# Modulation lines later, router rows turned without their gains, and six unread products between logits and first expert

## The reference

```python
mod_x = (jax.nn.silu(c) @ w_ada[l] + b_ada[l])[:, None, :]
sh_a, sc_a, g_a, sh_m, sc_m, g_m = jnp.split(mod_x, N_MOD, axis=-1)
...
x = x + g_a * _merge(ya, yb, ga, gb, w_oa[l], w_ob[l], w_out[l])
hx = _modulate(_rmsnorm(x, norm_mlp[l]), sh_m, sc_m)   # h * (1 + scale) + shift
x = x + g_m * moe(hx.reshape(b * s, d)).reshape(b, s, d)

def _moe(h, router_w, router_b, w_gate, b_gate, w_up, b_up, w_down, b_down):
    logits = (h @ router_w + router_b).astype(jnp.float32)
    top_logit, top_e = lax.top_k(logits, TOP_K)
    top_w = jax.nn.softmax(top_logit, axis=-1)
    ...
    gate = jnp.minimum(xe @ w_gate[e] + b_gate[e], SWIGLU_LIMIT)
    up = jnp.clip(xe @ w_up[e] + b_up[e], -SWIGLU_LIMIT, SWIGLU_LIMIT)
    act = (up + 1) * (gate * jax.nn.sigmoid(SWIGLU_ALPHA * gate))
    return act @ w_down[e] + b_down[e]
```

## Time and profile before

| | |
|---|---|
| median of three executions | 1819.28 us (1817.63 to 1820.83) |
| profiled execution | 1815.5 us |
| its span on the device | 1813.7 us |
| PE busy | 1748.5 us, 96% |
| DVE busy | 787.1 us, 43% |
| ACT busy | 571.7 us, 32% |
| DMA | 563.07 MB, mean 310 GB/s |
| chain that ended last | PE 77%, DMA 16%, DVE 4%, ACT 2% |

### The profile page before, as it was taken

How to read it: one execution, slowest core, us unless ns; L and a number is a source line. 1 busy time by engine, 2 the same in 40 slices (tenths; PEclk the granted TensorE clock), 3 DMA queues, 4 the chain that set the end, 5 groups by cost and what they waited for, 6 DMA issues and landing times.

```text
span 1813.7 us, 22741 instructions
## 1 busy us (share of the span) xinstructions
PE 1748.5 (96%) x9326; PEld 1032.5 (57%) x9326; DVE 787.1 (43%) x1419; ACT 571.7 (32%) x1034; POOL 20.6 (1%) x59
## 2 busy tenths in 40 slices
PE   6999999999999999999999999989999999999999
PEld 4988886333333333333332333348788888888887
DVE  3887964111111111111111111134677776767776
ACT  4546663101101101101010010135654446664443
POOL 1020010000000000000000000000000000000000
PEclk9999999999999999999999999999999999999999
DMA  8655478999999999999999999996235637425550
GB/s 319 232 199 211 174 286 332 414 430 431 430 431 430 431 430 431 429 432 429 431 430 431 431 431 430 431 390 226 102 137 205 212 119 276 139 94 186 186 198 34
DMA packets 122042, 563.07 MB, mean 310 GB/s; under 512 B 7216, under 2 KB 53424, under 8 KB 97360
## 3 DMA queue, kind: packets, MB, share of 16 engines
q1 hardware_dynamic: 121104, 558.70, 76.2%
q10 hardware_dynamic: 832, 2.89, 0.4%
HBM read 560.52 MB, written 1.05 MB: 310 GB/s over the span
## 4 chain that ended last, share of the span: by engine, by line
PE 77%; DMA 16%; DVE 4%; ACT 2%; issue 1%; SPq 0%; DVEq 0%; ACTq 0%
PE ps L1117 17%; PE ps L1140 10%; PE ps L1397 9%; PE ps L669 7%; PE ps L671 7%; PE ps L670 7%; DMA ring<-in_w_up 7%; DMA arena<-in_w_up 7%; PE ps L1398 4%; PE ps L1073 3%; PE ps L1054 3%; DVE part L2099 1%; DMA ring<-in_w_ada 1%; PE ps L994 1%; PE ps L1066 1%
## 5 line engine op out<-in xcount | busy, mean ns | idle before, releaser
L2099 DVE TENSOR_TENSOR part<-ring,part 128x1024 fp32r<-128x1024 f32 (+2 forms) x300 | 320.9, 1088 | 140.7 <-ACT part L1526 140.1
L669 PE MATMUL ps<-part,part 128*128 128x512 f32 (+1 forms) x888 | 312.5, 352 | 4.5 <-DVE part L2099 2.2
L671 PE MATMUL ps<-part,part 128*128 128x512 f32 (+1 forms) x888 | 301.9, 340 | 0.0
L670 PE MATMUL ps<-part,part 128*128 128x512 f32 (+1 forms) x888 | 301.8, 340 | 0.0
L1526 ACT ACTIVATE part<-ring 128x1024 fp32r<-128x1024 f32 (+2 forms) x299 | 272.9, 946 | 86.5 <-DVE ring L2099 69.6
L1117 PE MATMUL ps<-ring,arena 128*64 128x512 f32 x1216 | 268.3, 594 | 8.0 <-DMA ring<-in_w_up 8.0
L1397 PE MATMUL ps<-part,part 128*128 128x512 f32 x704 | 250.3, 398 | 0.0
L2096 DVE TENSOR_SCALAR arena<-ps 128x512 f32<-128x512 f32 x64 | 44.3, 692 | 421.2 <-PE ps L1117 421.2
L1398 PE MATMUL ps<-part,part 128*128 128x256 f32 x704 | 197.5, 281 | 0.0
L1117 PEld LDWEIGHTS ps<-ring,arena 128*64 128x64 f32 x1216 | 85.0, 137 | 188.1 <-issue 171.5
L669 PEld LDWEIGHTS ps<-part,part 128*128 128x128 f32 x888 | 168.3, 190 | 32.6 <-issue 7.8
(11 more groups left out here) (275 smaller groups left out, 1446.1 us busy)
## 6 DMA issues: line engine op xcount, KB each, us to landing
ring<-in_w_down SPq DMA_DIRECT2D x39, 2048.0 KB, 31.4
ring<-in_w_up SPq DMA_DIRECT2D x38, 2048.0 KB, 32.2
ring<-in_w_gate SPq DMA_DIRECT2D x38, 2048.0 KB, 31.4
arena<-in_w_up SPq DMA_DIRECT2D x26, 2048.0 KB, 33.7
ring<-in_ffn_w_in SPq DMA_DIRECT2D x44, 1024.0 KB, 7.6
arena<-in_w_down SPq DMA_DIRECT2D x18, 2048.0 KB, 32.6
spare<-in_w_gate SPq DMA_DIRECT2D x13, 2048.0 KB, 31.5
arena<-in_w_gate SPq DMA_DIRECT2D x13, 2048.0 KB, 31.4
```

The source lines that it names most:

```text
L669: e.matmul(out, x[0], y[0], start=first, stop=False, skip_group_check=True)
L670: e.matmul(out, x[0], y[1], start=False, stop=False, skip_group_check=True)
L671: return e.matmul(out, x[1], y[0], start=False, stop=last, skip_group_check=True)
L2099: return e.tensor_tensor(out, x, y, op)
```

## The change

Six things change, all before or at the start of the expert loop.

1. ada_first: slab 6 begins with block 14 instead of 11, slab 7 with 17 instead of 14, slabs 8 to 11 one block later each. ada_column stays.
2. The two heads of a unit share one operation for the negated maximum and one for the inverted sum; ACT waits once for the pair.
3. The rows of X are turned by PE without any gain (turn_x, 16 transposes of 128x128 by the identity), between the products of the out-projection. Scale and root are moved elsewhere: the router's weights are multiplied by the scale on DVE, the shift's part of the logits is made by eight products of its own (shift_logits) and added to the bias, and the logits are multiplied by root when they are picked. The products with the diagonal, the 16 turns into b.htok and their copies are gone.
4. Gathering takes X itself, with root in S instead of 1. Expert 0 is gathered as the others are, and its rows turned by transposes. Scale and shift are applied where the gathered rows leave PSUM, four instructions on ACT and four on DVE (gathered_right) for each expert, with gains laid out by 16 small products (slot_gains).
5. Six products which no instruction reads (stay_busy: identity times X into PS[2], 512 columns, the first 256) stand between the logits and the first expert's products.
6. mod and smcol are laid ahead of the ring, with a pad behind them, so that ring and arena move by 1,024 and 128 bytes a partition; the largest count is reduced after the selection for expert 0; a table of functions is loaded in block 36 for the logarithm and exponential in place of the square root, and the load of that table in the router goes.

```diff
-        ada_first = {4: 5, 5: 8, 6: 11, 7: 14, 8: 19, 9: 22, 10: 25, 11: 28}
+        ada_first = {4: 5, 5: 8, 6: 14, 7: 17, 8: 20, 9: 23, 10: 26, 11: 29}
...
-                for r in range(2):
-                    x = st(2 * u + r)
-                    e.wait_ge(*s_max.of("max", u, r))
-                    stt(x[1], x[0], -1.0, unit_rr(u, r), ALU.mult, ALU.mult).then_inc(*s_max.up(u, r))
+                e.wait_ge(*s_max.of("max", u, 1))
+                stt(st_pair(u, 1), st_pair(u, 0), -1.0, unit_rr(u, 0, 2), ALU.mult, ALU.mult).then_inc(*s_max.up(u))
...
+        mod = sb("mod", [128, 96])
+        smcol = sb("smcol", [128, 128])
+        sb("to_a_line", [128, -nc.sbuf_base % 256 // 4])
         ringt = sb("ring", [128, NSLOT, SLOT])
...
+            def turn_x(q, h):
+                e.wait_ge(*s_xn.of("a", q, h))
+                for k in range(4):
+                    n = 512 * h + 128 * k
+                    i = e.transpose(PS[b.x_bank[q, h]][:, 128 * k:128 * k + 128], X[:, q, n:n + 128], C("ident"))
+                i.then_inc(*s_ut.up("moe", q, h))
...
+                        if (q, h, k) == (0, 1, 4):
+                            shift_logits()
+                        if (q, h, k) == (1, 0, 7):
+                            e.wait_ge(*s_gm2.of("half", 1))
+                            e.wait_ge(*s_bdn.of(1))
+                            for half in range(2):
+                                turn_x(0, half)
+                        if (q, h, k) == (1, 1, 5):
+                            logits(0, range(8))
+                        if (q, h, k) == (1, 1, 7):
+                            turn_x(1, 0)
...
+            def stay_busy(*columns):
+                for n in columns:
+                    e.matmul(PS[2][:, 0:n], C("ident"), X[:, 0, 0:n], start=True, stop=True, skip_group_check=True)
+
+            logits(1, range(4))
+            stay_busy(256)
+            turn_x(1, 1)
+            stay_busy(512)
+            logits(1, range(4, 8))
+            slot_gains()
...
+            stay_busy(512, 512)
...
+            gather(0)
...
+                stay_busy(512)
+                turn_gathered(0)
+                turn_weights()
+                turn_places(0)
+                stay_busy(512)
...
-                    i = ts(S[:, CAP * q:CAP * q + CAP], C("iota", CAP), b.posK[:, q, ex:ex + 1], None, ALU.is_equal)
+                    i = ts(S[:, CAP * q:CAP * q + CAP], C("iota", CAP), b.posK[:, q, ex:ex + 1], b.root[q], ALU.is_equal, ALU.mult)
...
+                    for j in range(2):
+                        for h in range(2):
+                            at = 128 * j + CAP * h
+                            i = e.activation(b.xg[:, 4 * h + j, :], PS[b.xg_banks[ex][0]][:, at:at + CAP], ACT.Identity,
+                                             bias=b.slot[:, j, 1, h:h + 1], scale=b.slot[:, j, 0, h:h + 1])
```

More of the change, by code:

```diff
@@ L417, in build @@
         small_at[0] = 0
-        b.gm1 = tiny(8)
+        b.gains, b.slot = tiny(16), tiny(16).rearrange("p (j w h) -> p j w h", j=4, w=2)
+        b.gm1, b.shift = b.gains[:, 0:8], b.gains[:, 8:16]
+        b.root = [a.xstat[q][:, 2:3] for q in range(2)]
+        b.xg_banks = [(0, 3)] + [((6, 7), (4, 5))[ex % 2] for ex in range(1, NE)]
+        b.x_bank = {(0, 0): 2, (0, 1): 3, (1, 0): 1, (1, 1): 0}
         b.G2 = tiny(2 * NE)
@@ L882, in merged_part @@
+                i.then_inc(*s_gm.up("slot"))
             def merged_part(k, q):
@@ new lines, in scalar_program @@
+            row_squares(0, 0)
+            row_squares(0, 1)
+            for h in range(2):
+                x_turned(0, h)
+            row_root(0)
+            row_squares(1, 0)
+            x_turned(1, 0)
+            row_squares(1, 1)
+            row_root(1)
+            for q in range(2):
+                picked_exp(q)
+            e.wait_ge(*s_gm.of("slot"))
+            copy(b.slot, PS[1][:, 0:16].rearrange("p (j w h) -> p j w h", j=4, w=2)).then_inc(*s_gm2.up("slot"))
+            gathered(0)
```

294 lines of the change are left out of this document (140 added, 154 removed).

## The result

The changed kernel takes 1808.05 us (median of four executions, 1807.14 to 1809.62), the kernel before 1818.45 us beside it. The ratio is 0.9936 with a 95% interval of 0.9925 to 0.9948. The forecast had the sign and a range that holds the time, but its size was short: 7.4 us against 11.6 us by the ratio. The time lies near the lower end of that range (1807 to 1816.5 us), which was there for the case of faster arena loads. That case did not come, so it is luck that the range holds the time.

The account below looks back on a forecast made before the run. The experts end with their weight transfers, which hang on the first expert's start. Attention stage -6.9 and router -0.5 give -7.4 us from the median 1819.28, so 1811.9 us, range 1807 to 1816.5.

Parts of the forecast that it names:

- the case of faster arena loads: Rival: expert weight loads into arena slots gain 0.046 us each from the new alignment, -2.6 us, 1809.3 us; chance 0.10.
- The attention stage: Up to about 273 us: later modulation lines remove PE's hole and half-clock time, and blocks 25 to 30 lighten; -6.9 us.
- the 3.2 us for the spell: Half-clock time of PE from 119.5 us on, behind the 2.44 us hole, goes too; 3.2 us with the edges.
- The 0.7 us given to the merged statistics: Blocks 25 to 30: one operation per pair of heads for negated maxima and reciprocals saves 0.7 us in six blocks.
- the sign that named none: Sign of being right: blocks 25 to 30 without PE's waits of 0.3 to 0.7 us.
- The rival of another late link: At 117 us the clock falls anyway or another link is late; only 2 to 4 us come, 1815.5 us; chance 0.12.
- The router: From block 45's end to the first expert: rows turned plainly, work removed and added; start at 30.95 instead of 31.46, -0.5 us.
- slot_gains: Added router work before the first expert: 16 products of 32x4 in 32 instructions, taken as 2.1 us, bounds 1.1 and 3.4.
- So by these rows there is nothing to win back: Router, 297 to 301 us: granted clock stayed at 1.00, so unread products buy no clock and cost where they outlast waits.
- The difference goes over to the median: Whole kernel: profiled execution lies 3.8 us below the median of 1819.28; that gap carries over, so 1819.28 - 7.4 = 1811.9 us.
- E: Start of the first expert's products; whatever moves it moves the experts' end; from 304.86 to about 297.4 us.
- The layout: Arena slots moved onto a multiple of 256 bytes: taken as 0 us, upper bound 2.6 us for 57 arena loads.

Follow-up runs that it names:

- before_ada_2: Kernel before with only the new table ada_first (slabs 6 to 11 begun later), second run; ratio 0.9955, median 1811.80 us.
- after_third: The changed kernel, unchanged, run a third time for comparison on the same chip; ratio to the kernel before 0.9934, median 1808.00 us.
- before_fill: Kernel before with three unread products in PE's 2.4 us wait ahead of scores(1) at 117 us; ratio 0.9990, median 1819.84 us.
- before_again: The kernel before, unchanged, profiled once more; ratio 0.9992, median 1819.14 us.
- before_busy: Kernel before with six unread products in its own waits between the out-projection and the first expert; ratio 0.9980, median 1816.91 us.
- old_ada: The changed kernel with the old table ada_first put back; ratio to the kernel before 0.9976, median 1815.32 us.
- no_busy: The changed kernel without its six unread products; ratio to the kernel before 0.9950, median 1811.28 us.
- busy_early: The changed kernel with only the first two unread products, between the logits; ratio to the kernel before 0.9939, median 1807.87 us.
- after_again: The changed kernel, unchanged, profiled once more; ratio to the kernel before 0.9940, median 1807.61 us.
- old_layout: The changed kernel with mod and smcol behind the spare slot again and no pad; ratio to the kernel before 0.9937, median 1808.72 us.
- trimmed: The changed kernel with one of two unread products behind the places left out and the last two cut to 320 and 256 columns; ratio 0.9926, median 1807.24 us.
- trimmed_2: Second run of trimmed, the changed kernel with shorter unread products; ratio to the kernel before 0.9928, median 1807.34 us.
- trimmed_start: As trimmed, plus two unread products (512 and 256 columns) in PE's wait behind block 0; ratio to the kernel before 0.9940, median 1812.25 us.

## Why the prediction was short

**The attention stage was right, with one term by luck.** Forecast -6.9 us; the trace of before_ada_2, which has the table alone and no spell ahead of block 44, gives -6.5, and after_third, the whole change without such a spell, 268.72 - 262.47 = 6.25. The hole is gone, and so is the spell behind it, as the forecast supposed; before_fill shows that the idle time set it off. But the 3.2 us for the spell were read from one trace, where it lasts 6.8 us. In before_again, before_busy and old_ada it lasts 3.4 us, some 1.7 us of time, and in before_again a longer wait (1.41 us instead of 0.46 at 215 us) makes up for most of it. The 0.7 us given to the merged statistics did not come: the table alone leaves the same two waits, against the sign that named none. The rival of another late link did not occur.

**The router was mis-sized.** Forecast -0.5, measured -2.16. The term that was wrong is slot_gains: 2.1 us, from the row of products with 32 columns, and 0.67 us in the trace, which is under the estimate's lower bound of 1.1. Of this 1.4 us 0.2 became a wait for DVE's picks (the row at 290.53 us); some 1.2 us reached the first expert. The unread products outlast the selection as forecast: leaving one out and cutting two gave 0.9 us at the first expert.

**"So by these rows there is nothing to win back" failed.** The step read one execution's clock of 1.00 in 297 to 301 us as a property of the kernel. In before_again and before_fill the router runs at the lower level for 10.2 us, and only 10 of 78 executions have the 0.998 or more of the trace it rested on. The six products are worth 2.6 us in the change (no_busy), 3.6 in the kernel before (before_busy).

**"The difference goes over to the median" failed with it.** The 3.8 us between the profiled execution and the median were not a constant offset: they were half-clock time, 17 us in a mean execution beside 6.8 us in the profiled one; the traces that show more than that have 10.2 us of it in the router, and the change removes most of it. The two profiled executions are alike in this: ahead of its last 3 us each has 6.8 us at the lower level, the changed kernel 3.4 at 42.5 and 3.4 at 315.6 us. So their spans show mostly the shorter work and idle time, 6.2 us. At an equal clock of 0.998 the executions average 1816.0 (eight of before) and 1809.3 us (five of the change): 6.7 us of shorter work and idle time. The other 4.8 us of the 11.5 between the means (1819.75 and 1808.2) go with the clock's rise from 0.9953 to 0.9989.

**What held.** The end of the experts followed E: 6.27 us beside 6.94, with a spell of 3.4 us in the first expert for the difference (last section). E came at 297.92 us where 297.5 was named, although the attention stage brought 4.78 us in this trace and the router more than forecast, so that this match is chance. The first wait for a transfer did not come near 850 us but at 895.95 (before at 901.24). The layout was worth nothing. The evictions of gathered rows on two engines made no wait in the loop.

## What to carry to other kernels

A profile is one execution; before its clock row carries a term of a sum, its own time has to be set against the spread of the others, and a gap between them read as time at the lower level rather than as an offset. Short waits of PE in a row, of half a microsecond each, can cost microseconds through the clock besides the time they last: with the last four products left out the first expert starts 33.08 us behind block 44's products (busy_early), with all six left out 36.75 (no_busy). An unread product in the first of the waits paid here; it should end where the wait ends. Moving an engine's deferrable lines past the point where another engine needs its answer is worth the wait and the slow stretch behind it.

## What was not expected of the hardware

PE at the lower level is not always behind idle time. In the changed kernel a spell of 3.4 us began at 315.6 us in the first expert, and one near 313 or 314 us in the traces of after_again, old_layout and after_third, with PE's last idle time, 0.2 us, over 20 us earlier. Windows of 4 us in the changed kernel:

```profile
312.00:316.00 4.00, 4.00 (x10) 1.41 (x11) 2.34 (x3) 0.00 (x0) 0.00 (x0) 0.95 1.02 438
316.00:320.00 4.00, 3.83 (x14) 1.15 (x10) 0.00 (x0) 0.73 (x2) 0.00 (x0) 0.63 0.99 420
```

It costs 0.7 us or more at the end of the experts: from the first expert's products to the end of the last wait for a transfer it takes 890.9 to 891.2 us in these four traces, and 889.6 to 890.2 in old_ada, busy_early, trimmed and trimmed_2, which have no spell there. What sets it off is open. The six unread products do not prevent it. Of the four traces with fewer of them behind the places three lack it (busy_early, trimmed, trimmed_2) and trimmed_start has it, too few to tell from chance.

Also not expected: 32 instructions of slot_gains, products of 4 columns, took 0.67 us, 0.02 us each; the smallest product in the rows before, of 32 columns, took 0.07. They also write to four groups of 32 partitions in turn, which those do not; which of the two makes them quick is not shown.
